# Stage beginnings worked off by row tile: the crossings between the blocks of a three-block float32 network on one core

## What is computed

```python
def rmsnorm_2(x, g):                     # before every stage
    y = x * rsqrt(mean(x * x, axis=-1) + 1e-6)
def half_ffn(h, shift, scale, gate, g_pre, g_post, w13, w2):
    # u = norm(h) modulated; y = (silu(u @ w1) * (u @ w3)) @ w2
    # h + gate * norm(y)
h_lat = half_ffn(h_lat, ..., w13_a, w2_a)
h_lat, _ = token_mixing(h_lat, ...)
h_lat = half_ffn(h_lat, ..., w13_b, w2_b)
h = h + mla_mixer(rmsnorm_3(h, a_norm_g), ...)
h = h + rglru_mixer(rmsnorm_3(h, b_norm_g), ...)
```

## Time and profile before

| | |
|---|---|
| median of 3 runs | 2326.73 us (2322.61 to 2327.68) |
| profiled execution, time | 2324.72 us |
| its span, first to last instruction | 2323.3 us |
| PE busy | 1982.9 us (85%) |
| DVE busy | 1008.2 us (43%) |
| ACT busy | 735.3 us (32%) |
| POOL busy | 42.6 us (2%), 47 instructions |
| HBM read | 669 MB; some 400 GB/s until about 1330 us, then under 200 |

### The profile page before, as it was taken

The page is one execution under the profiler, slowest core; times in us unless marked ns, Lnnn a source line. Parts: engine busy times, 40 slices in busy tenths (PEclk is TensorE's granted clock), DMA queues, the critical chain, the costliest instruction groups (busy, mean ns, idle before and its releaser), DMA issues.

```text
span 2323.3 us, 28401 instructions
## 1 busy us (share of the span) xinstructions
PE 1982.9 (85%) x11830; PEld 1311.9 (56%) x11830; DVE 1008.2 (43%) x1713; ACT 735.3 (32%) x1196; POOL 42.6 (2%) x47
## 2 busy tenths in 40 slices
PE   6999777777877887777788799989999899999997
PEld 3556413332332433342444288868999788785786
DVE  3544222221221221222533367666664667653386
ACT  4333211111110111112111144454654554543365
...
GB/s 399 419 310 264 405 392 410 417 413 414 413 414 414 416 413 412 416 411 408 410 410 409 405 188 192 168 102 170 112 143 175 165 178 185 95 203 19 145 118 19
DMA packets 210432, 672.03 MB, mean 289 GB/s; under 512 B 11504, under 2 KB 134512, under 8 KB 152192
## 3 DMA queue, kind: packets, MB, share of 16 engines
...
...
## 4 chain that ended last, share of the span: by engine, by line
PE 50%; DMA 34%; DVE 11%; ACT 4%; issue 2%; SPq 0%; POOL 0%; DVEq 0%; ACTq 0%
DMA ring<-in_w 24%; PE pb L231 7%; PE pb L239 7%; PE pb L232 7%; PE pb L233 7%; DMA ring<-in_w_a 6%; PE pb L240 4%; DMA ring<-in_w_in 3%; DVE WB L333 3%; PE pb L1844 3%; PE pb L774 2%; PE pb L1869 2%; ACT WB L327 1%; DMA ring<-in_w_mod 1%; PE pb L3149 1%
## 5 line engine op out<-in xcount | busy, mean ns | idle before, releaser
L333 DVE TENSOR_TENSOR WB<-ring,WB 128x1024 fp32r<-128x1024 f32 (+3 forms) x370 | 426.1, 1193 | 465.4 <-ACT WB L327 465.1
L327 ACT ACTIVATE WB<-ring 128x1024 fp32r<-128x1024 f32 (+3 forms) x370 | 361.6, 1026 | 800.0 <-DMA ring<-in_w_a 463.3
L1844 PE MATMUL pb<-ring,big 128*32 128x512 f32 x2048 | 300.3, 679 | 147.1 <-DMA ring<-in_w 131.5
L231 PE MATMUL pb<-HHL,WB 128*128 128x256 f32 (+1 forms) x976 | 292.8, 300 | 11.8 <-DVE WB L333 4.3
L232 PE MATMUL pb<-HHL,WB 128*128 128x256 f32 (+1 forms) x976 | 284.2, 291 | 0.0
L233 PE MATMUL pb<-HHL,WB 128*128 128x256 f32 (+1 forms) x976 | 283.8, 291 | 0.0
L239 PE MATMUL pb<-HHL,WB 128*128 128x512 f32 x704 | 253.5, 404 | 1.7 <-DVE tmpT L643 1.4
L1844 PEld LDWEIGHTS pb<-ring,big 128*32 128x32 f32 x2048 | 46.8, 114 | 364.0 <-DMA ring<-in_w 275.3
L231 PEld LDWEIGHTS pb<-HHL,WB 128*128 128x128 f32 x976 | 195.1, 200 | 35.9 <-issue 20.6
L1869 PE MATMUL pb<-ring,big 128*32 128x512 f32 x1024 | 163.6, 649 | 49.5 <-DMA ring<-in_w 41.7
L240 PE MATMUL pb<-HHL,WB 128*128 128x256 f32 x704 | 198.9, 283 | 0.0
...
## 6 DMA issues: line engine op xcount, KB each, us to landing
ring<-in_w SPq DMA_DIRECT2D x384, 1024.0 KB, 16.5
...
ring<-in_w_mod SPq DMA_DIRECT2D x24, 1024.0 KB, 11.6
...
```

The source lines that it names most:

```text
L231: pe.matmul(o, l[0], r[0], start=start, stop=False)
L327: act.activation(WB[:, c % 2, 0, x:y], flat[:, x:y], ACT.Copy).then_inc(*A(("high", c, z)))
L333: dve.tensor_tensor(WB[:, c % 2, 1, x:y], flat[:, x:y], WB[:, c % 2, 0, x:y].bitcast(F32), ALU.subtract).then_inc(*V(("low", c, z), *([("f ...
L1844: e = pe.matmul(PB[half][32 * j:32 * j + 32, :], xeT[:, kk, 32 * x:32 * x + 32], s[:, 512 * j:512 * j + 512], start=kk == 0, stop=kk == 7)
```

## The change

Five edits.

1. **Row products tile by tile.** `pe_rows` gets `tail=4`: the last four slices (two chunks) are kept together. All four are done for the first row tile, then all four for the next. The waits for the low halves and for the operands stand at each slice of the first tile in the order. The chunk before the last is free only in the last tile's pass.
2. **Crossings by row tile.** `act_cross` and `dve_cross` interleave the end of one stage and the beginning of the next: post-processing, norm, transposes and the high and low parts of row tile 0, then those of row tile 1. Each piece is 128 columns wide; four pieces share one high and one low instruction (128x4x128). The low parts of pieces 0 to 3 are DVE's, of 4 to 7 POOL's.
3. **First chunks of a stage.** The high halves of nine chunks (`CROSSING`, mostly the first and the second chunk of each stage) are written by ACT between the steps of the crossing, and their low halves by POOL instead of DVE.
4. **First products by row tile.** In `pe_half`, PE does chunk 0 for tile 0, transposes tile 1, then chunk 1 for tile 0, chunk 0 for tile 1, chunk 1 for tile 1. "mx", "a3" and "b3" are ordered alike. Where the tokens are the moving operand (both halves, the gates of "mx", "b3"), each matmul is done once for each tile.
5. **Norms** at "xf", "b3" and "out" take their squares in halves, on ACT and DVE, tile by tile.

```diff
-    def both_columns(pe, bank, hi, lo, kk):
-        pe.matmul(bank[:, :].rearrange("p (z t) -> p z t", z=2), hi, HHL[:, :, kk, 0:256], start=kk == 0, stop=False)
-        return pe.matmul(bank[:, 0:256], lo, HH[:, kk, 0:256], start=False, stop=kk == 7)
+    def both_columns(pe, bank, hi, lo, kk, x=0, n=256):
+        pe.matmul(bank[:, :].rearrange("p (z t) -> p z t", z=2)[:, :, x:x + n], hi, HHL[:, :, kk, x:x + n], start=kk == 0, stop=False)
+        return pe.matmul(bank[:, x:x + n], lo, HH[:, kk, x:x + n], start=False, stop=kk == 7)
...
+    CROSSING = (s_ffa + 1, s_mix, s_mix + 1, s_ffb, s_ffb + 1, s_3, s_3 + 1, s_3 + 12, s_3 + 13)
...
+    def pool_split_half(pool, c, z):
+        x, y = halves_at(CH[c][1])[z]
+        pool.wait_ge(*at("high", c, z))
+        pool.tensor_tensor(WB[:, c % 2, 1, x:y], slot(("s", c))[:, x:y], WB[:, c % 2, 0, x:y].bitcast(F32), ALU.subtract).then_inc(
+            *G(("low", c, z), *([("free", ("s", c))] if z else [])))
...
-            if n == nk - 2:
+            if nk - tail <= n < nk - 1:
                 continue
...
+    def pool_turn2(pool, name, c, c0=0):
+        for z in range(2 if c in CROSSING else 0):
+            pool_split_half(pool, c, z)
+        low2(pool, G, name, 0, 1, c0)
+        for z in range(2):
+            pool_split_half(pool, c + 1, z)
+        low2(pool, G, name, 1, 1, c0)
...
+        act_ready(act)
+        squares(0, 1)
+        squares(0, 0)
+        root(0)
+        act_squares2(act, name, 0, xn(0)[:, 0:512], [("added", post, 0, 0)])
+        act_split_half(act, c, 0)
+        act_root2(act, name, 0)
+        act_scale2(act, name, xn, 0)
+        act_split_half(act, c, 1)
+        squares(1, 1)
+        squares(1, 0)
+        root(1)
+        act_turned2(act, name, 0, c0)
+        act_split_half(act, c + 1, 0)
+        act_squares2(act, name, 1, xn(1)[:, 0:512], [("added", post, 1, 0)])
+        act_split_half(act, c + 1, 1)
+        act_root2(act, name, 1)
+        act_scale2(act, name, xn, 1)
+        act_turned2(act, name, 1, c0)
...
         product(0, 0)
         product(0, 1)
...
+        add(0)
+        dve_squares2(dve, name, 0, xn(0)[:, 512:1024])
         product(1, 0)
+        dve_scale2(dve, name, xn, 0)
         product(1, 1)
...
+        dve_turned2(dve, name, 0, a, s, c0)
+        add(1)
+        dve_squares2(dve, name, 1, xn(1)[:, 512:1024])
+        dve_scale2(dve, name, xn, 1)
+        dve_turned2(dve, name, 1, a, s, c0)
...
+        pe_turn2(pe, name, F.xn, 0)
+        first(0, 0)
+        pe_turn2(pe, name, F.xn, 1)
+        first(0, 1)
+        first(1, 0)
+        first(1, 1)
...
+        pe_turn2(pe, "mx", lambda i: xn_m[:, i, :], 0)
+        first(0)
+        first_rows(0)
+        pe_turn2(pe, "mx", lambda i: xn_m[:, i, :], 1)
+        first(1)
+        first_rows(1)
...
+        pe_turn2(pe, "b3", xn3, 0)
+        pe.wait_ge(*at("XT", "b3", "meta"))
+        first_columns(0, 0, 144)
+        pe_turn2(pe, "b3", xn3, 1)
+        first_columns(1, 0, 144)
+        first_columns(0, 144, 272)
+        first_columns(1, 144, 272)
```

450 lines of the change are left out of this document (245 added, 205 removed).

## The result

| | before | after |
|---|---|---|
| median | 2327.20 us (4 runs, 2322.61 to 2328.91) | 2383.17 us (4 runs, 2375.84 to 2385.81) |
| profiled execution, time | 2324.72 | 2384.20 |
| ratio | | 1.0248 (95% interval 1.0231 to 1.0265) |

The changed kernel is slower by 56 us; the forecast was 34 us more (2361), with a range up to 2373. The direction was right, the time lies outside the range.

What follows compares the result with a forecast made beforehand. Expert weight transfers were taken to bound the kernel until some 1330 us, then PE, except at crossings. Terms 5 + 6 + 7.5 + 2 + 14 + 1.4 = 35.9 us on the profiled 2324.72 gave 2360.6, forecast 2361, range 2340 to 2373.

Steps and rivals of the forecast that it cites:

- "b3"'s term: Crossing into "b3": 192 narrower matmuls at 0.12 us, 10.8 more, and later operands; +14 us (+5 to +17).
- tile 1's chain: At "fb": tile 1's addition, square, root, scaling done at T+27; T is ACT's start on the last chunk's highs.
- The floor: PE at clock 1.00: a matmul below 256 moving columns costs what 256 cost, 0.12 us.
- Rival 1: No floor: 128 columns cost half at clock 1.00, so tile 1's chain ends last; 2344 us, chance 0.15.
- The clock: PE at the crossings: clock 0.50 for the first 5 us, as before.
- "fb": Crossing into "fb": first two chunks done for both tiles at T+39.3, before T+34.0; +5 us (+3 to +8).
- Tile 0's chain: Crossing into "fb": tile 0's steps up to the first product, at T+20.3 where it was T+20.8.
- "mx": Crossing into "mx": doubled gates' matmuls and later tile 1 tokens, at F+14 from first product F; +7.5 us (+5 to +10).
- "fa" and "a3": Crossings: "fa" +6 us (+4 to +8), PE work as in "fb" and a later norm; "a3" +2 (0 to +4).
- The end: Last row product, "wob": five slices left after the last operand instead of four; +1.4 us.
- Rival 2: POOL goes ahead of DVE's three two-input steps for tile 1, holding each up to 2.4 us; 2372, chance 0.07.
- Rival 3: Crossings: tile 0's first product before T+16 keeps PE working at clock 1.00; -17 us, 2308, chance 0.06.

Runs made afterwards that it cites:

- the kernel with PE kept at work: Changed kernel with identity transposes added in up to three of PE's holes at each crossing; 2371.73 us, ratio 1.0203.
- the second trace: The changed kernel run once more, unaltered, and profiled again; 2383.91 us, ratio 1.0260.

## Why the prediction was right or wrong

- **Where the miss lies.** The direction was right, the size too small: 35.9 us forecast, 59.5 and 57.3 in the two traces. Of the 23.6 missing in the first, 9.6 are its first block, 6.6 "mx", 3.2 "b3", 3.1 "fb" and 1.4 the end; of the 21.4 in the second, 17.1 are "b3", 3.0 "fb", 1.5 "mx" and 1.1 the first block, less 1.8 in "fa". So the steps that failed are the clock in "b3"'s term and, by less, tile 1's chain.
- **The floor.** Right. 0.23 for a pair, 0.11 for a matmul of 144 columns at clock 1.00; with the clock at 1.00 "b3" costs 14.9 by the trace of the kernel with PE kept at work, forecast 14. Rival 1 fell. Yet with the doubling in "b3" undone its cost was still 11.8, where rival 1 had tile 1's chain there at 5: the wait for tile 1 is nearly as long as the doubled work that lay over it. The Trainium skill ("TensorE: Matmul & The Clock Gate", section "Wait — 56ns, not 53.3ns?") gives 55.6 ns for 128 columns at full clock; for these two-part float32 operands the trace has twice that, and the measurement decides.
- **The clock.** This is the step that failed most. The sum took "clock 0.50 for the first 5 us as before" for every crossing, and "b3"'s term priced all 192 matmuls at 0.12, with no low clock at all. There it was 13.5 us in one trace and 47.4 in the other, 3.4 before. That is 3 of the missing us in the first trace, and 17 in the second. In "fb" a second stretch of 3.4 us comes with the idle time ahead of tile 1's transposes (in both traces), and "mx" has 23.9 and 17.0 us at 0.50, where it was 10.2 before; "fa" and "a3" have one stretch as before. Filling PE's holes gave back 12 us in all, part of it in "b3".
- **"fb".** Tile 0's chain was right within 0.6 us and the wait before the third slice within 0.2. Tile 1's tokens came at T+28.2 instead of T+27: the additions at 4.65 and the square at 2.74 (0.69 alone), where the sum took 1.5 of the 4.1 us that POOL could cost. With the second low stretch that made +8.1 instead of +5 (8.0 in the second trace), at the upper end of the range given (+3 to +8).
- **"mx".** +14.1 and +9.0 instead of +7.5. Besides the clock the first trace shows a wait that the sum did not have, in ACT's queue for the second chunk (the first line), and tile 1's gates at F+14.9, where F+14 was forecast (F is 1555.58 here):

```profile
1557.58 1.06 ACT L329 ACTIVATE WB<-ring 128x1024 fp32r<-128x1024 f32 x1 [2.08 <-DMA ring<-in_w_in]
...
1570.45 0.44 PE L231 MATMUL pb<-HHL,WB 128*128 128x128 f32 x1 [2.99 <-DVE HHL L666]
```

  The second trace has the same wait (2.18), and there tile 1's gates came at F+14.0 (1559.12, F 1545.12). What the wait costs alone was not tried. With products over both tiles the four traces scatter by 1 us here and not by 8, so the scatter too comes with the narrow gates' matmuls or with the order around them.
- **"fa" and "a3".** Right within 2 us in both traces by the table; with the 2.5 us by which the reference trace's "fa" is slow, "fa" was 2.7 and 0.7 above its 6.
- **The end.** +2.8 and +1.3, forecast +1.4. In the kernel before, four slices cost 1.2 there, which is the forecast's term. In the changed kernel they cost 2.6, and 1.5 more with the low clock, and the norms in halves give 1.2 to 1.4 back, which the forecast had at 0. That the second trace has just the forecast's figure is luck.
- **The first block.** The forecast said the change touches little there, and that holds; the first trace's 9.6 us are its execution's.
- **Rival 2** (POOL goes first, +11) was right as a mechanism: POOL held DVE's steps for tile 1, and low halves on DVE take 9 us away. By its times the forecast lay nearer: T+28.2 is between the T+27 of the sum and the T+29.6 of the rival, so part of the rival's 11 us was in the result beside the clock. **Rival 3** failed where the forecast said it would, at DVE's second product of tile 1. What no rival had is a clock that stays low while PE works.
- **Slips in the sums.** The items of "b3" add up to 14.7 (13.7 and 1 for the row product), taken as 14. The lower bounds of the places add up to 18.4, which gives 2343 and not 2348. Neither changes the outcome.
- **The range** took the clock as a constant. Its upper end needed one case more, "b3" entirely at half speed: 192 matmuls at 0.21 are 40 us, 17 more than the 23.0 of the forecast.
